# A product with ones takes over an addition: eight chunks summed as seven plus one

## What is computed

```python
def layer_norm(x):
    mu = jnp.mean(xf, axis=-1, keepdims=True)
    var = jnp.mean(jnp.square(xf - mu), axis=-1, keepdims=True)
    return ((xf - mu) * lax.rsqrt(var + EPS)).astype(x.dtype)

def post_norm(x, y):
    return layer_norm(ALPHA * x + y)
...
xl = post_norm(xl, 0.5 * g1 * swiglu(modulate(xl, sh1, sc1), ffn1_w_in[l], ffn1_w_out[l]))
```

## Time and profile before

| what | value |
|---|---|
| median of 3 runs | 2040.81 us (2040.19 to 2041.56) |
| the profiled execution | 2039.96 us |
| its span, first to last instruction | 2038.2 us |
| TensorE matmul busy | 2017.8 us (99%) |
| TensorE weight load busy | 1756.9 us (86%) |
| VectorE busy | 1360.9 us (67%) |
| ScalarE busy | 754.4 us (37%) |
| GpSimd busy | 158.0 us (8%) |

### The profile page before, as it was taken

The page is one execution under the profiler, slowest core; times in us unless marked ns, Lnnn a source line. Parts: engine busy times, 40 slices in busy tenths (PEclk is TensorE's granted clock), DMA queues, the critical chain, the costliest instruction groups (busy, mean ns, idle before and its releaser), DMA issues. The chain is left out here.

```text
span 2038.2 us, 30134 instructions
## 1 busy us (share of the span) xinstructions
PE 2017.8 (99%) x12733; PEld 1756.9 (86%) x12733; DVE 1360.9 (67%) x2107; ACT 754.4 (37%) x944; POOL 158.0 (8%) x138
## 2 busy tenths in 40 slices
PE   9999999999999999999999999999999999999998
PEld 8979979888888988788888888988888899879998
DVE  6966976776785668657876785655555475477565
ACT  4464465222122544535222213522122252465333
POOL 0500500000002000020000002000000210010001
PEclk9999999999999999999999999999999999999999
DMA  6654654554543310223454543333432234214553
GB/s 247 236 173 142 240 181 158 188 195 173 197 169 119 117 45 6 101 91 131 182 194 166 206 161 121 142 125 109 177 148 108 98 129 165 81 43 166 184 187 105
DMA packets 68769, 300.89 MB, mean 148 GB/s; under 512 B 6176, under 2 KB 23200, under 8 KB 48672
## 3 DMA queue, kind: packets, MB, share of 16 engines
q1 hardware_dynamic: 65920, 290.06, 39.6%
q10 hardware_dynamic: 2720, 8.99, 1.2%
HBM read 297.97 MB, written 1.05 MB: 147 GB/s over the span
## 5 line engine op out<-in xcount | busy, mean ns | idle before, releaser
L503 PE MATMUL PS<-xh,wh 128*128 128x512 f32 (+1 forms) x3660 | 991.2, 347 | 1.0 <-issue 0.5
L503 PEld LDWEIGHTS PS<-xh,wh 128*128 128x128 f32 x3660 | 654.2, 188 | 90.1 <-DVE wh L410 1.3
L503 PE MATMUL PS<-xl,wh 128*128 128x512 f32 (+1 forms) x2070 | 699.9, 338 | 0.0
L406 ACT ACTIVATE wh<-raw 128x2048 fp32r<-128x2048 f32 (+4 forms) x219 | 373.5, 1706 | 303.8 <-PE PS L503 227.4
L410 DVE TENSOR_TENSOR wh<-raw,wh 128x2048 fp32r<-128x2048 f32 (+3 forms) x181 | 371.9, 2055 | 96.5 <-ACT wh L406 96.1
L503 PEld LDWEIGHTS PS<-xl,wh 128*128 128x128 f32 x2070 | 388.8, 188 | 43.5
L503 PE MATMUL PS<-HH,wh 128*128 128x512 f32 (+1 forms) x1276 | 347.1, 358 | 0.3 <-DVE wh L410 0.2
L1378 DVE CUSTOM_DVE_ANT_0 NRM<-SQ,CBR 128x1024 f32<-128x1024 f32 x240 | 284.0, 1221 | 5.8
L1299 ACT ACTIVATE SI<-PS 128x512 f32<-128x512 f32 (+1 forms) x88 | 48.0, 545 | 580.0 <-PE PS L503 566.1
L503 PEld LDWEIGHTS PS<-HH,wh 128*128 128x128 f32 x1276 | 227.1, 188 | 37.2 <-DVE wh L410 1.2
L503 PE MATMUL PS<-HL,wh 128*128 128x512 f32 (+1 forms) x638 | 228.4, 358 | 0.0
(11 more groups left out here) (432 smaller groups left out, 2395.7 us busy)
## 6 DMA issues: line engine op xcount, KB each, us to landing
raw<-ffi_dram SPq DMA_DIRECT2D x88, 1024.0 KB, 4.9
SQ<-adat_dram SPq DMA_DIRECT2D x120, 512.0 KB, 3.6
raw<-ffo_dram SPq DMA_DIRECT2D x64, 704.0 KB, 4.2
raw<-layer_dram SPq DMA_DIRECT2D x36, 1024.0 KB, 5.0
lent<-layer_dram SPq DMA_DIRECT2D x14, 1024.0 KB, 7.5
raw<-odd_dram SPq DMA_DIRECT2D x12, 1024.0 KB, 4.9
raw<-even_dram SPq DMA_DIRECT2D x9, 1024.0 KB, 4.8
raw<-eout_dram SPq DMA_DIRECT2D x4, 1024.0 KB, 4.9
```

What stands on the lines that cost most here:

```text
L406: act.activation(high(i)[:, 0:n], raw[:, i.slot, 0:n], ACT.Copy).then_inc(hi_done, 1)
L503: m = pe.matmul(out, w[rows, o:o + P], x, start=n == 0 and j == 0, stop=n == len(tiles) - 1 and j == 2)
```

## The change

After stages 0, 2 and 3 the addition of chunk 7 (`sum_seventh`) is gone in both halves. In its place a new function `column_sums_apart` multiplies the seven-chunk sums in `NRM` with ones and then chunk 7 of X and SQ with ones, accumulating into the same columns of bank 5 and bank 7. TensorE waits on `ln_in` for the first and on the semaphores of the addition and the square of chunk 7 for the second. The counting of `ln_all` is renumbered, since only four units still use it.

```diff
+        SUMMED = [norm_unit(1, 0), norm_unit(1, 1), norm_unit(4), norm_unit(5)]
+        def seventh_ready(m, h):
+            i = end_slabs(m)[1][0]
+            return (drained[i.par], i.d // 2 + 1) if h else (on["half_added"], 2 * m + 2)
+        def column_sums_apart(pe, m, h, tiles):
+            cols = lambda t: slice(t * P, (t + 1) * P)
+            for j in range(2):
+                pe.wait_ge(on["ln_in"], SUMS_IN[m] + 2 * h + 1 + j)
+                for t in tiles:
+                    pe.matmul(PS[:, 5 + 2 * j, cols(t)], NRM[:, j, cols(t)], ones, start=t == tiles[0], stop=False, skip_group_check=True)
+            ready = (seventh_ready(m, h), (on["ln_sq"], SQUARES[m] + len(whole_slabs(m)) + 2 * h + 2))
+            for j, src in enumerate((X, SQ)):
+                pe.wait_ge(*ready[j])
+                for t in tiles:
+                    mm = pe.matmul(PS[:, 5 + 2 * j, cols(t)], src[:, 7, cols(t)], ones, start=False, stop=True, skip_group_check=True)
+                mm.then_inc(on["ln_sum"], 1)
...
         def column_sums(pe, u, tiles):
             for j in range(2):
-                pe.wait_ge(on["ln_all"], 2 * u + j + 1)
+                pe.wait_ge(on["ln_all"], 2 * SUMMED.index(u) + j + 1)
...
# pair_in_halves (late half) and pe_end_halves (early half)
-                    column_sums(pe, late, (2, 3))
+                    if m == 2:
+                        column_sums(pe, late, (2, 3))
+                    else:
+                        column_sums_apart(pe, m - 1, 1, (2, 3))
...
-            column_sums(pe, u, (0, 1))
+            if m == 1:
+                column_sums(pe, u, (0, 1))
+            else:
+                column_sums_apart(pe, m, 0, (0, 1))
...
# dve_end_halves: only for m == 1 now
-            sum_seventh(dve, m, 0)
+                sum_seventh(dve, m, 0)
...
-                sum_seventh(dve, m, 1)
+                    sum_seventh(dve, m, 1)
```

## The result

| | median of 22 runs | lowest |
|---|---|---|
| before | 2041.61 us | 2040.19 |
| changed | 2045.28 us | 2044.18 |

The ratio is 1.0020, 95% interval 1.0014 to 1.0026. The whole interval lies above no change, and its middle lies on the 0.2% that was named as what can be told. The forecast was +3.8 us (2044.6); the medians differ by 3.67 us. The median of before over these 22 runs is 0.8 us above that of the three runs from which the forecast started.

A forecast was written before the change was run, and what follows sets the result against it. TensorE, busy 99%, was taken to bound the kernel. Early halves +2.70 us and late halves +1.16 us made +3.86, said as +3.8, on the 2040.81 us median: 2044.6 us, range 2042.9 to 2046.5.

The forecast's parts named there:

- An added product costs 0.225 us: TensorE's stream: each added f32 128x128 product with ones costs 0.225 us, 0.90 us per half, 5.4 us for 24.
- The early half is paid in full: Sums for columns 0 to 255: no new wait and no gain, +0.90 us per stage change, 2.7 us in three.
- The late half costs 0.40, 0.36 and 0.40 us: Sums for columns 256 to 511, inside the first pair of slabs: added products less the vanished xl stall, 1.16 us together.
- Behind the late mean nothing, or up to +0.1 us each: Next xl after VectorE's late mean: new TensorE stall at most 0.1 us per stage change, taken as nothing.
- The sum of +3.8 us: Whole kernel: early halves 2.70 plus late halves 1.16 us, +3.86, said as +3.8, giving 2044.6 us.
- The range: Whole kernel time: from 2042.9 us (0.35 us less per half) to 2046.5 us (late stall kept, plus a new one).
- VectorE's idle time: VectorE in the changed stage changes: idle some 2 us before the early mean, about 1 us before the late one.
- The span of 2042.0: Profiled execution of the changed kernel: span near 2042.0 us, from 2038.2 before.
- the late stall stays: Late half: VectorE's saving misses xl, products cost whole 5.4 up to 5.7 us; time 2046.2 to 2046.5; chance 0.17.
- partly hidden by TensorE's free 14%: Early half: stalls for xl swallow its products too, 2.3 us back in three stage changes, time 2042.3; chance 0.15.
- Faster: First pairs of slabs: early products free and late xl stall gone, 1.5 us less, 2039.3 us; chance 0.03.

The follow-up runs named there:

- experiment 2: Kernel before with eight products and no additions in the three early halves only; 2044.71 against 2041.44 us, ratio 1.0018.
- experiment 4: Kernel before, VectorE additions kept, each of the four products with ones done twice at the six groups; 2045.82 against 2041.44 us, ratio 1.0020.
- experiment 5: Changed kernel, unaltered, run again against before; 2044.99 against 2041.42 us, ratio 1.0018.
- experiment 8: 16 of 128 columns of ones, in the changed kernel (2046.91 us, ratio 1.0022) and in one with late sums issued earlier (2040.87 us, 0.9993).
- narrow: Changed kernel with 16 of 128 columns of ones in all products with ones; 2046.91 against 2041.65 us for before, ratio 1.0022.
- the control: Kernel before, unchanged, run a second time; 2041.50 against 2041.44 us, ratio 0.9998.

## Why the prediction was right, step by step

- *An added product costs 0.225 us.* Measured 0.89 / 4 = 0.222 us at each of the three early groups, in the changed kernel and in experiments 2, 4 and 5. The four passes of which the Trainium skill speaks (FP8 and Floating Point Precision, TensorE Precision Notes) gave an estimate of 213 ns for 128 columns, and give one of 427 ns for 256. The trace agrees with both, at 222 ns and at two records of 216. With 16 columns the estimate is 27 ns, and there experiment 8 has 222 ns: a floor that at 128 columns happens to lie where the passes do. TensorE: Matmul & The Clock Gate, section LDWEIGHTS, of the Trainium skill gives a load as columns / 1.2 ns, an estimate of 107 ns for 128 columns. It fits the 0.11 us from record to record, and that a narrower moving side changes nothing; the load records of these products themselves last 0.19 us and overlap.
- *The early half is paid in full.* Right; +0.89 us each, and experiment 2 by itself gives +3.3 us. It was built on two readings: TensorE came 0.4 us after the last addition (669.00 against 668.56), so nothing waited for it; and all that follows hangs on TensorE's own sums.
- *The late half costs 0.40, 0.36 and 0.40 us.* Measured +0.37, +0.34 and +0.37. Right in size. One of its two reasons was not needed: the prediction let `xl` come sooner because the additions left VectorE's queue. It does come sooner, but with the additions kept (experiment 4) the stall goes too. The stall can be filled by a longer group or removed by a shorter queue, 0.4 to 0.5 us either way, and only once. The change did both and got one.
- *Behind the late mean nothing, or up to +0.1 us each.* It went the other way, -0.13 us each, which is the small wait and slower pace that before had at that place. The late mean was read 1.53 us after the group's start (683.47 - 681.94), as worked out (1.54), so the chain was no later than the bound allowed.
- *The sum of +3.8 us.* The aligned records have 3.61, the medians 3.67 and 3.57. That these lie so near is in part luck: the groups and what follows them directly give 3.35 us, the 0.40 us given back was not in the sum, and steps of tenths and the clock fill most of the difference.
- *The range.* Its low end does not follow from its own words: 0.35 us less in each of six halves is 2.1 us less than 3.86, so 1.76 us more than before and 2042.6 us. The 2042.9 takes the 2.1 us as what is added. The result lies far from either.
- *VectorE's idle time.* "Some 2 us" before the early mean was 2.90: the 0.9 us of products and the freed additions both add to the 1.09 us of before, and I counted one. "About 1 us" before the late one was 0.64. The prediction's own times give 0.72: it had `xl` done at 680.98, held by `xh`, and the sum out at 681.70. Neither changes the time.
- *The span of 2042.0.* It was 2044.1 in that execution: 0.9 us before the change's first place and 1.2 us of reduced clock.

The rivals: "the late stall stays" fell in the trace of the changed kernel; "partly hidden by TensorE's free 14%" fell too, since the wait in front of the late group is 0.62 us in both and the early products cost all of their time. That the share of the weight loads is 86% said nothing of these groups, in which the loads follow each other without a gap. "Faster" needed products of a price that did not occur.

What stays open is the clock. The stretch at 755 us is in three of the twelve profiles, and all three are of kernels with eight full products in all six groups. The fourth profile of such a kernel, narrow, has 1.00 there, and so have the eight others. Six of the twelve profiles have such a stretch somewhere, and the one at 288 us lies before any changed instruction, so it does not need the change.

The mean granted clock that is on record for every execution says a little more. In the profiles, 0.998 stands only where such a stretch lies inside the run, 1.000 only where none does, and 0.999 with and without one. Before, over the three groups and the control, has 0.998 in 29 of 98 executions and 1.000 in 46; the changed kernel, over its two groups, has 0.998 in 11 of 33 and 1.000 in one. So executions at 0.998 are as common in both, but the changed kernel's clock is a little lower on the whole, by some 0.0005. With 1.2 us for a stretch that lowers the mean by 0.0008, that is an estimate of at most 0.7 us in the medians; between them and the 3.35 us of the records lie 0.3 us. Whether it is the change that lowers it is not settled; it was not tried to move TensorE's thin stretch at 751 to 753 alone. If it came with every execution, the medians would show 3.6 + 1.2 = 4.8 us, and they show 3.6 and 3.7, so at the most it comes with some.

## What to carry to other kernels

Moving work from an engine with slack to the engine that sets the pace costs its full price, unless it lands in a wait of that engine; before pricing what is saved, look whether anyone was waiting for it. A stall can be paid for once: count the cover it gives to the longer group or to the shorter queue, not to both. And when small work must sit on the busy engine, look one or two instructions up and down its stream for a gap: the same eight products cost +0.36 us in one place and -0.42 us in the other.

## What the runs showed of the hardware

- An f32 product whose stationary tile changes each time shows as two records and costs 0.222 us, with 128 columns on the moving side (1.70 us for a group of eight) as with 16 (1.70 us). With 256 columns (L1030) the records are 0.216 us apart.
- Two products that open columns in one bank and two that add to them later cost no more than products that open and close at once: 1.70 us for both (changed kernel, experiment 4).
- The granted clock fell to 0.50 for some three microseconds at 755 us in a kernel that was otherwise at full clock on one core, behind a stretch of few products, with no idle time of TensorE in the rows; it cost 1.2 us. In other executions the same instructions ran on at 1.00, and such a stretch stood elsewhere (288, 926, 1848 us) or nowhere.
